# Four row-group products per expert in place of one product per quad of experts

## The reference

```python
for layer in range(2):
    x = x + mixer(rmsnorm(x, norm[layer]))          # layer 0: HGRN2 + NSA heads; layer 1: sliding window attention
    x = x + hier_moe(rmsnorm(x, moe_norm[layer]))
# hier_moe: top-1 group of 4, top-2 experts of the 8 in it, weights w;
# each token: y = sum over its 2 experts e of w_e * (silu(h @ w_gate[e]) * (h @ w_up[e])) @ w_down[e]
```

## Time and profile before

| | us |
|---|---|
| median of 3 runs (1213.69 to 1215.48) | 1215.11 |
| the profiled execution's own time | 1214.79 |
| its span | 1213.0 |
| PE busy in the span | 891.5 |
| DVE / ACT busy | 338.6 / 186.4 |
| bytes moved, mean rate | 440.79 MB, 363 GB/s |

### The profile page before, as it was taken

How to read it: one execution, slowest core, us unless ns; L and a number is a source line. 1 busy time by engine, 2 the same in 40 slices (tenths; PEclk the granted TensorE clock), 3 DMA queues, 4 the chain that set the end, 5 groups by cost and what they waited for, 6 DMA issues and landing times.

```text
span 1213.0 us, 27990 instructions
## 1 busy us (share of the span) xinstructions
PE 891.5 (73%) x12510; PEld 638.6 (53%) x12510; DVE 338.6 (28%) x867; ACT 186.4 (15%) x470; POOL 28.6 (2%) x34
## 2 busy tenths in 40 slices
PE   6999998787665757575757989677757666666665
PEld 5666764664544535454545565655545444444453
DVE  1376454232121212121214562421202121111111
ACT  3323432010000000000003352111001000000000
POOL 2121000000000000000000000000000000000000
PEclk9999998999888888888889999799979798988788
DMA  9846135899999999999999742899999999999995
GB/s 398 331 165 243 70 139 208 340 407 425 429 428 430 427 429 430 427 429 427 430 427 429 297 175 79 317 411 428 427 429 427 428 428 428 430 426 430 428 430 250
DMA packets 31148, 440.79 MB, mean 363 GB/s; under 512 B 3584, under 2 KB 3712, under 8 KB 4480
## 3 DMA queue, kind: packets, MB, share of 16 engines
q1 hardware_dynamic: 30528, 438.32, 86.3%
q10 hardware_dynamic: 576, 1.83, 0.4%
HBM read 439.09 MB, written 1.05 MB: 363 GB/s over the span
## 4 chain that ended last, share of the span: by engine, by line
DMA 54%; PE 35%; DVE 5%; ACT 3%; issue 2%; SPq 1%; DVEq 0%; ACTq 0%
DMA side<-weights 45%; PE PS L456 11%; DMA ring<-weights 8%; PE PS L797 7%; PE PS L787 5%; PE PS L464 2%; PE PS L767 2%; DVE side L1194 1%; PE PS L807 1%; PE PS L491 1%; PE PS L526 1%; SPq L289 1%; ACT side L1013 1%; DVE scr L1194 1%; DVE st L1408 1%
## 5 line engine op out<-in xcount | busy, mean ns | idle before, releaser
L787 PE MATMUL PS<-ring,probT 128*32 128x128 f32 x5120 | 172.5, 294 | 78.4 <-DMA ring<-weights 70.7
L787 PEld LDWEIGHTS PS<-ring,probT 128*32 128x32 f32 x5120 | 153.0, 119 | 96.8 <-DMA ring<-weights 82.7
L787 PE MATMUL PS<-side,probT 128*32 128x128 f32 x3072 | 125.3, 330 | 87.6 <-DMA side<-weights 82.4
L787 PEld LDWEIGHTS PS<-side,probT 128*32 128x32 f32 x3072 | 108.3, 134 | 111.6 <-DMA side<-weights 102.0
L456 PE MATMUL PS<-ring,side 128*128 128x512 f32 (+1 forms) x352 | 148.2, 574 | 2.4 <-ACT side L920 1.4
L1194 DVE TENSOR_TENSOR scr<-scr,PS 128x128 f32<-128x128 f32 x64 | 18.4, 288 | 411.4 <-ACT scr L1121 411.4
L1624 DVE COPY probT<-PS 32x256 f32<-32x256 f32 x128 | 54.3, 424 | 189.8 <-PE PS L797 188.9
L456 PEld LDWEIGHTS PS<-ring,side 128*128 128x128 f32 x352 | 65.3, 190 | 70.1 <-issue 69.3
L797 PE MATMUL PS<-side,scr 128*32 128x256 f32 x1024 | 78.6, 457 | 32.0 <-DMA side<-weights 26.8
L797 PE MATMUL PS<-ring,scr 128*32 128x256 f32 x1024 | 71.4, 425 | 24.1 <-DMA ring<-weights 14.2
L1125 ACT ACTIVATE probT<-PS 32x256 f32<-32x256 f32 x128 | 47.8, 374 | 256.6 <-PE PS L797 255.8
(11 more groups left out here) (215 smaller groups left out, 680.7 us busy)
## 6 DMA issues: line engine op xcount, KB each, us to landing
ring<-weights SPq DMA_DIRECT2D x128, 2048.0 KB, 34.5
side<-weights SPq DMA_DIRECT2D x80, 2048.0 KB, 27.2
x<-x_in SPq DMA_DIRECT2D x2, 512.0 KB, 4.1
out<-x SPq DMA_DIRECT2D x2, 512.0 KB, 2.7
TB<-table ACTq DMA_DIRECT2D x1, 973.5 KB, 11.3
SM<-small ACTq DMA_DIRECT2D x1, 732.0 KB, 17.6
TB<-table ACTq DMA_DIRECT2D x1, 64.0 KB, 3.8
SM<-small ACTq DMA_DIRECT2D x1, 20.0 KB, 4.7
```

The lines of the kernel that those rows point to most:

```text
L787: mm = pe.matmul(PS[f * CAP:(f + 1) * CAP, b, up * P:(up + 1) * P], gatherT[:, k, tok], w[:, k, f * P:(f + 1) * P], start=(k == 0), stop=( ...
```

## The change

The down results stay where PE writes them: `yq` becomes [128, 4 experts, 256], written by one ACT copy per expert, with the output quarter q on partitions 32q to 32q+31. The combining product is done per expert, on 32 rows of PE for each quarter, into four banks (0, 1, 6, 7) that sum over the quad's experts. For this `pickT` must hold each expert's 32 rows four times over, on every group of partitions: 32 products with the identity in place of two transposes, into banks 4 and 5, and one ACT copy of 128 x 1024 (it lies now where a table of layer 0's mixer was). The gather writes banks 2 and 3. DVE adds four 128 x (2 x 256) pieces to `x`; `m_acc` counts quarters of the columns and not token tiles, and the output goes out in four DMAs. The next quad's `pick` is made after the second expert's work.

```diff
@@ SP, the end of the program @@
-            for t in range(TT):
-                sp.wait_ge(m_acc[t], end1 * 2)
-                sp.dma_start(out[t * P:(t + 1) * P, :], x[:, t, :]).then_inc(stored, 16)
+            for q in range(4):
+                sp.wait_ge(m_acc[q], end1)
+                sp.dma_start(out[:, q * 256:(q + 1) * 256].rearrange("(a p) n -> p a n", p=P),
+                             x[:, :, q * 256:(q + 1) * 256]).then_inc(stored, 16)
@@ PE, transposes of x for layer 1 (ACT's norm: m_acc[3]) @@
-                    pe.wait_ge(m_acc[t], iters * 2)
+                    pe.wait_ge(m_acc[2 * half + 1], iters)
@@ PE, quad @@
+                def turn_picks():
+                    pe.wait_ge(m_pick, i + 1 + layer)
...
+                    for e in range(QE):
+                        for t in range(TT):
+                            c = (e * TT + t) * P
+                            for q in range(4):
+                                tr = pe.matmul(PS[q * CAP:(q + 1) * CAP, 4 + c // 512, c % 512:c % 512 + P],
+                                               pickw[:, t, e * CAP:(e + 1) * CAP], ident, start=True, stop=True)
+                    tr.then_inc(m_pickw_turned, 1)
+                def combine(e):
+                    pe.wait_ge(m_y, QE * i + e + 1)
...
+                    for t in range(TT):
+                        for q in range(4):
+                            r = slice(q * CAP, (q + 1) * CAP)
+                            mm = pe.matmul(PS[:, OUT_BANK[q], t * 256:(t + 1) * 256], pickT[r, e, t * P:(t + 1) * P],
+                                           yq[r, e, :], start=(e == 0 and t == 0), stop=(e == QE - 1),
+                                           skip_group_check=True)
+                            if (e, t) == (QE - 1, TT - 1):
+                                mm.then_inc(m_comb, 1)
...
-                    if half == 0:
-                        pe.wait_ge(m_pick, i + 1 + layer)
-                        for t in range(TT):
-                            tr = pe.transpose(PS[:, 2, t * P:(t + 1) * P], pickw[:, t, :], ident)
-                        tr.then_inc(m_pickw_turned, 1)
-                pe.wait_ge(m_pickT, i + 1)
...      (after the gate and up products of expert e)
+                    if e == 0:
+                        turn_picks()
+                    else:
+                        combine(e - 1)
                     pe.wait_ge(m_hid, QE * i + e + 1)
                     pe.transpose(PS[:, b, 2 * P:3 * P], hid[:, e % 2, :], ident).then_inc(m_hid_turned, 1)
                     w = moe_landed(layer, i, 3 * e + 2).rearrange("p (f n) -> p f n", f=4)
+                    if e == 0:
+                        pe.wait_ge(m_pickT, i + 1)
...      (after the last expert)
-                pe.wait_ge(m_y, 2 * QE * i + 2 * QE)
-                for n in range(4):
-                    t, half = n // 2, n % 2
-                    if n >= 2:
-                        pe.wait_ge(m_acc[0], 2 * i + n - 1)
-                    pe.matmul(PS[:, 6 + n % 2, :], pickT[:, t * P:(t + 1) * P],
-                              yq[:, half * 512:(half + 1) * 512], start=True, stop=True).then_inc(m_comb, 1)
+                combine(QE - 1)
@@ ACT, quad @@
-                act.wait_ge(m_pickw_turned, i + 1)
-                act.activation(pickT[:, :], PS[:, 2, 0:S], ACT.Copy).then_inc(m_pickT, 1)
...      (after expert 0's silu)
+                        act.activation(pickT[:, :, :].rearrange("p e t -> p (e t)"), banks(4, 2),
+                                       ACT.Copy).then_inc(m_pickT, 1)
...
-                    for q in range(2):
-                        ins = act.activation(yq[e * CAP:(e + 1) * CAP, q * 256:(q + 1) * 256],
-                                             PS[q * CAP:(q + 1) * CAP, 4 + e % 2, 0:256], ACT.Copy)
-                    ins.then_inc(m_y, 1)
+                    act.activation(yq[:, e, :], PS[:, 4 + e % 2, 0:256], ACT.Copy).then_inc(m_y, 1)
@@ DVE, quad (its two copies of the down result go; pick_quad moves behind expert 1) @@
-                    xs = x[:, n // 2, (n % 2) * 512:(n % 2 + 1) * 512]
-                    tt(xs, xs, PS[:, 6 + n % 2, :], ALU.add).then_inc(m_acc[n // 2], 1)
+                    xs = x[:, :, q * 256:(q + 1) * 256]
+                    tt(xs, xs, PS[:, OUT_BANK[q], :].rearrange("p (a n) -> p a n", a=TT), ALU.add).then_inc(m_acc[q], 1)
```

More of the change, by code:

```diff
@@ L179, in build @@
         pick, pickw = scr6[:, 3, :, :], scr6[:, 4, :, :]
-        pickT = scr[:, 5 * S:6 * S]
+        pickT = TB[:, TABLE["lvl"][0]:TABLE["lvl"][0] + QE * S].rearrange("p (e t) -> p e t", e=QE)
+        assert TABLE["lvl"][0] + QE * S <= TABLE["window"][0]
+        OUT_BANK = (0, 1, 6, 7)
         def buffer(n):
@@ L244, in build @@
         m_silu, m_hid, m_hid_turned, m_hidT = sem("m_silu"), sem("m_hid"), sem("m_hid_turned"), sem("m_hidT")
-        m_y, m_comb, m_acc = sem("m_y"), sem("m_comb"), [sem(f"m_acc{t}") for t in range(TT)]
+        m_y, m_comb, m_acc = sem("m_y"), sem("m_comb"), [sem(f"m_acc{q}") for q in range(4)]
         m_onehot, m_lowered = sem("m_onehot"), sem("m_lowered")
@@ L760, in quad @@
             def quad(layer, i):
+                def turn_picks():
+                    pe.wait_ge(m_pick, i + 1 + layer)
+                    if not started:
+                        pe.wait_ge(m_y, QE * i)
+                    for e in range(QE):
[8 more added lines that the diff above has]
+                    if e == 0:
+                        pe.wait_ge(route_ready, layer + 1)
+                        if not started:
+                            pe.wait_ge(m_acc[3], i)
+                    for t in range(TT):
[6 more added lines that the diff above has]
+                                mm.then_inc(m_comb, 1)
+                started = isinstance(i, int) and i == 0
                 pe.wait_ge(m_onehot, i + 1 + layer)
@@ L766, in quad @@
                             d = 4 * half + k
-                            mm = pe.matmul(PS[:, half, k * P:(k + 1) * P], xn[:, t, d * P:(d + 1) * P],
+                            mm = pe.matmul(PS[:, 2 + half, k * P:(k + 1) * P], xn[:, t, d * P:(d + 1) * P],
                                            pick[:, t, :], start=(t == 0), stop=(t == TT - 1))
                     mm.then_inc(m_gathered, 1)
-                    if half == 0:
-                        pe.wait_ge(m_pick, i + 1 + layer)
-                        for t in range(TT):
-                            tr = pe.transpose(PS[:, 2, t * P:(t + 1) * P], pickw[:, t, :], ident)
-                        tr.then_inc(m_pickw_turned, 1)
-                pe.wait_ge(m_pickT, i + 1)
                 for e in range(QE):
@@ L1611, in quad @@
                     dve.wait_ge(m_gathered, 2 * i + half + 1)
-                    tt(gatherT[:, 4 * half:4 * half + 4, :], PS[:, half, :].rearrange("p (k c) -> p k c", k=4),
+                    tt(gatherT[:, 4 * half:4 * half + 4, :], PS[:, 2 + half, :].rearrange("p (k c) -> p k c", k=4),
                        last(g[:, 4 * half:4 * half + 4], P), ALU.mult).then_inc(m_gatherT, 1)
-                pick_quad((i + 1) % QUADS, i + 2 + layer)
                 for e in range(QE):
@@ L1620, in quad @@
                     dve.tensor_copy(hidT[:, e % 2, :], PS[:, b, 2 * P:3 * P]).then_inc(m_hidT, 1)
-                    dve.wait_ge(chunk_done, DONE_MOE[layer] + 3 * e + 3 + QC * i)
-                    for q in range(2, 4):
-                        ins = dve.tensor_copy(yq[e * CAP:(e + 1) * CAP, q * 256:(q + 1) * 256],
-                                              PS[q * CAP:(q + 1) * CAP, 4 + e % 2, 0:256])
-                    ins.then_inc(m_y, 1)
-                for n in range(4):
-                    dve.wait_ge(m_comb, 4 * i + n + 1)
-                    xs = x[:, n // 2, (n % 2) * 512:(n % 2 + 1) * 512]
-                    tt(xs, xs, PS[:, 6 + n % 2, :], ALU.add).then_inc(m_acc[n // 2], 1)
+                    if e == 1:
+                        dve.wait_ge(m_pickw_turned, i + 1)
+                        pick_quad((i + 1) % QUADS, i + 2 + layer)
+                for q in range(4):
+                    dve.wait_ge(m_comb, 4 * i + q + 1)
+                    xs = x[:, :, q * 256:(q + 1) * 256]
+                    tt(xs, xs, PS[:, OUT_BANK[q], :].rearrange("p (a n) -> p a n", a=TT), ALU.add).then_inc(m_acc[q], 1)
             def experts(layer, first):
```

9 lines of the change are left out of this document (6 added, 3 removed).

## The result

The changed kernel takes 1232.09 us (median of 4 runs, 1227.15 to 1233.49), the kernel before 1215.30 beside it (4 runs, 1213.69 to 1216.58): a ratio of 1.0132, 95% interval 1.0115 to 1.0148. It is slower by 1.3%, 15 us over the forecast and 8.6 above the range. The profiled execution of the changed kernel took 1232.55 with a span of 1230.8, 17.8 longer than the span before.

A forecast was written before the change was run, and what follows sets the result against it. The prediction took the expert stages to be bound by weights arriving at 425 to 430 GB/s. From the profiled 1214.79 us, first quads +5.6 and ends -3.3 gave 1217.1, range 1210.5 to 1223.5.

The forecast's parts named there:

- Bounds and places: Expert stages wait for weights; PE, ACT and DVE changes show only in each layer's first quad and at its experts' end.
- second holes: Gap in the weight stream at each first quad's end, until SP's next loads; in layer 0 at 252 us.
- Combine: Per-expert combining product on PE: 0.97 us with row groups sharing PE, each costing 0.2 where PE idled 0.79.
- the second rival: Combine's row groups don't run side by side: 3.9 us each, 1237 in all; chance 0.04 unshared, 0.05 partly shared.
- turn_picks: Products turning the picks in the first quad: first down product 3.0 us behind gate and up, before 1.6; cost 1.4.
- Gather: First quad: two transposes leave the gather's middle, so the first chunk is used 0.4 us earlier.
- Delivery in the first quads: Fetching the added PE instructions ahead of chunk 12 costs 1.5 us per layer, bounds -4.0 and +5.
- the twelfth chunk: First quad's weight chunk whose use lets SP issue further loads; predicted 3.1 us later in layer 0, 2.5 in layer 1.
- the outer bound of +5 for delivery: First quad: +5 us if every instruction block needs 6.8 us; the range took the delivery bounds halfway.
- first rival: Delivery costs nothing more and the ends win: 1210.6, or 1209 with the last down product at full clock; chance 0.24.
- The loop's code: Third rival: the longer round no longer stays, each round is fetched, mostly hidden; 1222; chance 0.07.
- The ends: Behind each layer's last down product (end: T), last add at T + 3.9, before T + 5.56; -1.3 layer 0, -2.0 layer 1.

The follow-up runs named there:

- e9: Kernel before plus 56 two-column products that nothing reads (112 instruction pairs) in each layer's first quad; 1219.60 us, ratio 1.0042.
- e1: Changed kernel plus 28 idle PE instructions (waits already met) between layer 0's router products and its first quad; 1219.09 us, ratio 1.0030.
- e4: Changed kernel with each layer's first quad alone in the old form, the loops in the new form; 1221.59 us, ratio 1.0051.
- e5: Kernel before plus 120 one-column products (480 instructions) in each round of layer 0's loop, 1871 instructions a round; 1224.53 us, ratio 1.0056.
- e6: e1 with all four combining products of each layer's first quad put at the quad's end; 1212.45 us, ratio 0.9973.
- e3: Kernel before plus 102 one-column products (408 instructions) in each round of layer 0's loop, 1799 instructions a round; 1217.95 us, ratio 1.0024.
- e2: Kernel before plus 84 one-column products (336 instructions) in each round of layer 0's loop, 1727 instructions a round; 1215.60 us, ratio 1.0003.
- e8: e4 plus 80 idle PE instructions ahead of layer 1's first quad; 1215.50 us, ratio 0.9994.
- e7: e1 with the turning of the picks and all combining products of each first quad behind its last expert; 1214.61 us, ratio 0.9981.
- e10: Kernel before plus five long products of 128 rows and 512 columns (10 instruction pairs) in each layer's first quad; 1218.38 us, ratio 1.0028.
- e12: The same program as e6, run again; 1212.95 us, ratio 0.9994.

## Why the prediction was wrong

- *Bounds and places.* Right. The stream is full elsewhere, all of the loss is behind the two second holes and in layer 0's loop, and SP's loads follow the last down product one for one (259.38 and 830.59).
- *Combine.* 1.15 at full clock for 0.97 taken, and 0.3 on the path for 0.2. The row groups run side by side; the second rival is out.
- *turn_picks.* The first down product starts 2.94 behind the gate and up (3.0 taken). Right.
- *Gather.* 0.4 earlier was taken; it came 0.25 later in layer 0 and 0.8 earlier in layer 1 (6.15 for 5.90, 5.13 for 5.94), with a clock of 0.50 and 0.71 in the gather's first 5 us, where it had been 0.60 and 0.59.
- *Delivery in the first quads.* This term failed in size: +1.5 was taken, so +3.1 and +2.5 for the twelfth chunk, and it was +6.6 and +5.5, about what the outer bound of +5 for delivery gives (6.6 and 6.0), of which I had put only half into the range. The stops themselves grew by only 0.5 and 1.6, so as a price for stops 1.5 was not far off. What the sum lacks is the clock: PE's busy time grew by 8.6 and 6.8, of which the turning (1.9) and three combines (3 x 1.08, starts being spaced so) are 5.1, less the 0.4 of the two transposes that left. The other 3.9 and 2.1 go for the most part with the lower granted clock (0.74 to 0.92 behind 239 in layer 0, 0.66 for the last down product in layer 1, which took 3.53), as in e9; in layer 0 the gather has a part in it too. I had written the clock down only as a possible gain at the end (first rival).
- *The loop's code.* This failed outright. I gave it 0.07 and, if it came, +4, saying that fetching 48 us of a round's 58 would be hidden. It came in layer 0 and cost 9.1 in that layer's loop. The rival's own mechanism holds: the stops are hidden, PE still waits for weights in every round, and what costs is the traffic. Its price was wrong, 1.6 for the traffic and up to 2.4 at the end. It spread the packets' bytes over all engines; in the trace the last part of a load, which releases PE, went from +6.0 to +15.4, which is the 9.1, while the first part lost nothing. The sentence that failed is "In the steady stretch nothing is fetched": it told that the old round of 1391 instructions stays, and nothing of 1628 at another place in its packets. With that, 0.07 was too little; e1, e4 and e5 show that the place decides.
- *The ends.* T + 4.14 for T + 3.9. In layer 0 the gain of 1.4 was lost before layer 1's gather (+0.2): the sixteen records of the transposes wait for the adds between the first four and the rest, and took 3.76 (2.04 before the change) at a clock of 0.78. In layer 1 -1.4 for -2.0: the store was not faster, 3.1 from the last add to the end of the span as before: in the trace's slices its pieces of 1 KB moved at 305 to 373 GB/s, the old ones of 4 KB at 389 to 451. Not in the sum: -2.5 ahead of that end, 1.6 of it the last down product at full clock (1.93 for 3.55), as the first rival had it.
- *The sum.* First quads 5.6 predicted, 12.1 measured; loop 0, +9.1; ends and clock -3.3, -3.7; start +0.3.

What would have shown it: the instructions in a round, and the place of its head in a packet, counted from the old trace's stops, against the largest round known to stay. That was 1391, so it would have told of a risk and not of the result.

## What to carry to other kernels

A hardware loop whose body is near the size of PE's instruction store has a cliff: count the instructions of a round, and where in a packet its head falls, before adding to it, and again after every edit ahead of it, as an edit elsewhere can push it over or back (28 idle instructions were worth 13 us here in the median, 8.4 between the two traces). Fetched code shares the DMA engines with the data, so look at the last part of a load and not at the mean rate, which fell by 1% here. Code that runs for the first time beside a full weight stream can cost by its number of instructions even where PE has idle time for them: put as few as can be ahead of the event that restarts the stream. Such a stop can be paid twice, in itself and in the clock of what follows.

## What the runs showed of the hardware

- Products of 32 rows on four row groups, each into a bank of its own, run side by side: eight of 256 columns in 1.15 us, and four such sets in a row in 3.74 (e6, 64 records), 0.93 each.
- Tiny products: 64 records of two columns in 0.98 us over four column groups in turn (0.015 each), 67 of one column in 2.26 in one column group (0.034 each, e3). Going round four groups was twice as fast as staying in one.
- The granted clock fell to its lower level (1.2 GHz) for a stretch behind the gather in 14 of the 16 first quads with added instructions, and in 2 of the 12 in the old form (kernel before, e2, e3, e4, e5, e8). A stop for code isn't needed for it: in e3's layer 1, an old quad with no stop at all, PE waited 5.20 for weights and its last down product then took 3.64. Nor does a stop always bring it: the old quad's stop of 2.42 was followed by 1.00, and so were layer 0's in e7 and e10. It also differs between executions: e12 is the program of e6 and its first quads are 0.8 and 1.5 us longer. What decides it stays open.
- Instruction packets delay single parts of a load: with the code of a loop fetched again each round, first and last part of a 2 MB load drifted apart from 2.1 to 12.9 us over 78 loads in the changed kernel's layer 0, and to 12.9 again in e4's layer 1. Where nothing was fetched the distance stayed as it was (4.3 before the change, 1.9 in e1).
- PE's stop at a head that is fetched again was 5.1 to 5.8 us, beside weights at 423 to 427 GB/s; a stop in straight code 0.2 to 3.0.
